# Second block's bias table: rows shifted by a skewed DRAM read in place of a matmul with an exchange matrix

## The reference, cut to what matters

```python
qi = jnp.arange(BLOCK)[:, None]
kj = jnp.arange(2 * BLOCK)[None, :]
dist = qi + BLOCK - kj
bias = rel_bias.astype(jnp.float32)[t5_causal_bucket(dist)]   # (128, 256, 8 heads)
logits = jnp.where(mask, logits + bias, NEG_INF)
```

## Time and profile before

| | |
|---|---|
| median of 3 runs | 2342.88 us |
| the profiled execution's own time | 2340.86 us |
| its span, first to last instruction | 2339.1 us |
| mean granted TensorE clock | 0.995 of full speed |
| PE busy (matmul) | 2297.5 us, 98% of the span |
| DVE busy | 1256.0 us, 54% |
| POOL busy | 859.8 us, 37% |
| ACT busy | 839.3 us, 36% |
| DMA, mean over the span | 93 GB/s |

### The profile page before, as it was taken

The page is one execution under the profiler, slowest core; times in us unless marked ns, Lnnn a source line. Parts: engine busy times, 40 slices in busy tenths (PEclk is TensorE's granted clock), DMA queues, the critical chain, the costliest instruction groups (busy, mean ns, idle before and its releaser), DMA issues.

```text
span 2339.1 us, 28137 instructions
## 1 busy us (share of the span) xinstructions
PE 2297.5 (98%) x11073; PEld 1881.6 (80%) x11073; DVE 1256.0 (54%) x1571; ACT 839.3 (36%) x1014; POOL 859.8 (37%) x200
## 2 busy tenths in 40 slices
PE   7999999999999999999999999999999998999998
PEld 6889777888888888887768888887888777888887
DVE  6677445554436745774455643468555653630533
ACT  5333435332232242333353323222335644422332
POOL 1332223334444443221333444444442333443443
PEclk9999999999999999999999999999999999999999
DMA  6333133454445544331334444445783334444442
GB/s 149 84 68 66 37 73 72 91 107 91 97 100 113 153 104 90 73 69 40 72 70 87 96 96 101 90 111 144 159 168 73 72 73 90 90 90 90 101 106 72
DMA packets 193145, 218.05 MB, mean 93 GB/s; under 512 B 14608, under 2 KB 165272, under 8 KB 192408
## 3 DMA queue, kind: packets, MB, share of 16 engines
q1 hardware_dynamic: 192856, 216.63, 42.3%
q10 hardware_dynamic: 192, 0.05, 0.0%
HBM read 206.92 MB, written 9.73 MB: 93 GB/s over the span
## 4 chain that ended last, share of the span: by engine, by line
PE 49%; issue 34%; POOL 8%; DVE 4%; DMA 1%; SPq 1%; ACT 1%; DVEq 1%; POOLq 0%; ACTq 0%
PE psG L363 15%; PE psG L365 15%; PE psG L364 15%; POOL w_lo L2751 8%; PE psH L650 3%; DMA raw<-in_w_in_dram 1%; SPq L1950 1%; DVE tab L1687 0%; DVE sq L453 0%; PE psH L2142 0%; ACT w_hi L356 0%; PE psH L675 0%; PE psH L2106 0%; DVE s L1687 0%; DMA raw<-in_w_down_dram 0%
## 5 line engine op out<-in xcount | busy, mean ns | idle before, releaser
L2751 POOL TENSOR_TENSOR w_lo<-raw,w_hi 128x2048 fp32r<-128x2048 f32 x184 | 853.0, 4636 | 1459.9 <-ACT w_hi L356 1388.0
L363 PE MATMUL psG<-h_hi,w_hi 128*128 128x512 f32 x1648 | 652.6, 396 | 12.0 <-DVE h_lo L500 7.9
L356 ACT CAST w_hi<-raw 128x2048 fp32r<-128x2048 f32 x184 | 351.0, 1908 | 827.0 <-PE psG L365 797.3
L364 PE MATMUL psG<-h_lo,w_hi 128*128 128x512 f32 x1648 | 643.6, 391 | 0.0
L365 PE MATMUL psG<-h_hi,w_lo 128*128 128x512 f32 x1648 | 643.2, 390 | 0.0
L363 PEld LDWEIGHTS psG<-h_hi,w_hi 128*128 128x128 f32 x1648 | 310.4, 188 | 96.4 <-issue 28.7
L365 PEld LDWEIGHTS psG<-h_hi,w_lo 128*128 128x128 f32 x1648 | 310.3, 188 | 65.6
L364 PEld LDWEIGHTS psG<-h_lo,w_hi 128*128 128x128 f32 x1648 | 310.7, 189 | 64.2 <-issue 1.4
L2688 DVE TENSOR_TENSOR hq<-r 128x512 f32<-128x512 f32 x32 | 84.9, 2691 | 148.8 <-ACT r L2459 148.8
L363 PE MATMUL psG<-hid_hi,w_hi 128*128 128x512 f32 x352 | 138.0, 392 | 1.7 <-POOL w_lo L2751 1.7
L365 PE MATMUL psG<-hid_hi,w_lo 128*128 128x512 f32 x352 | 137.0, 389 | 0.0
(11 more groups left out here) (476 smaller groups left out, 3276.7 us busy)
## 6 DMA issues: line engine op xcount, KB each, us to landing
raw<-in_w_in_dram SPq DMA_DIRECT2D x121, 512.0 KB, 6.4
raw<-in_w_gate_dram SPq DMA_DIRECT2D x44, 512.0 KB, 5.9
raw<-in_w_up_dram SPq DMA_DIRECT2D x44, 512.0 KB, 6.5
raw<-in_w_down_dram SPq DMA_DIRECT2D x32, 512.0 KB, 6.2
raw<-in_w_ff_in_dram SPq DMA_DIRECT2D x32, 512.0 KB, 6.3
raw<-in_w_ff_out_dram SPq DMA_DIRECT2D x32, 512.0 KB, 5.9
raw<-in_w_o_dram SPq DMA_DIRECT2D x16, 512.0 KB, 5.7
raw<-in_w_down_dram SPq DMA_DIRECT2D x16, 384.0 KB, 5.3
```

The costliest lines, as they stand in the source:

```text
L356: act.copy(w_hi[:, s, :], raw[:, s, :]).then_inc(hi_done.sem, 1)
L363: pe.matmul(out, a_hi, b_hi, start=first, stop=False)
L364: pe.matmul(out, a_hi, b_lo, start=False, stop=False)
L2751: pool.tensor_tensor(w_lo[:, s, :], raw[:, s, :], w_hi[:, s, :].bitcast(F32), ALU.subtract)\
```

## The change

The vector is written to DRAM 128 times per head, once for each query row, and the table is read out of that with a row step one word shorter than a row (383 floats in place of 384), so that each row starts one word earlier in the vector. This gives the rows in the right order. The exchange matrix, the read into `t5_up`, the matmuls, the copies and the store of `bias_d` are gone, and with them SP's wait for the small store. The load of `bias` in the second block becomes four DMAs of 256 KB with pieces of 1 KB, in place of two of 512 KB with pieces of 2 KB.

```diff
@@ memory
-    exch = sb("exch", [P, P])
-    t5_dram = nc.dram_tensor("t5_dram", (QH, 3 * P), F32, kind="Internal").ap()
+    t5_dram = nc.dram_tensor("t5_dram", (QH, P, 3 * P), F32, kind="Internal").ap()
-    bias_d = nc.dram_tensor("bias_d", (P, QH * 2 * P), F32, kind="Internal").ap()
-    t5_up = hat("t5_up", 16, [P, QH, 2 * P])
-    bias_s = hat("bias_s", 24, [P, QH, 2 * P])
@@ tables_sync
         if l == 0 and u == 3:
             sp.wait_ge(made_dve.sem, T5_OK)
-            sp.dma_start(t5_dram, t5_rows[:, :]).then_inc(st_t5.sem, 16)
-            sp.wait_ge(st_t5.sem, 16)
-            with nc.allow_non_contiguous_dma(reason="overlapping rows"):
-                sp.dma_start(t5_up[:, :, :], bass.AP(t5_dram.tensor, 0, [[1, P], [3 * P, QH], [1, 2 * P]]))\
-                  .then_inc(ld_t5.sem, 16)
-        if l == 0 and u == 6:
-            sp.wait_ge(made_act.sem, BIAS_OK)
-            sp.dma_start(bias_d, bias_s[:, :, :].rearrange("p h k -> p (h k)")).then_inc(st_bias.sem, 16)
+            sp.dma_start(t5_dram, t5_rows[:, :].unsqueeze(1).broadcast_to([QH, P, 3 * P])).then_inc(st_t5.sem, 16)
@@ tables_stored (ACT, u == 8)
-            act.wait_ge(st_bias.sem, 16)
+            act.wait_ge(st_t5.sem, 16)
@@ tables_pe
         if l == 0 and u == 3:
             pe.wait_ge(ld_c.sem, 64)
-            pe.wait_ge(made_act.sem, BIAS_OK)
...
-        if l == 0 and u == 2:
-            pe.wait_ge(consts.sem, 8)
-            pe.wait_ge(ld_t5.sem, 16)
-            pe.wait_ge(made_dve.sem, ROW_OK)
-            for n in range(4):
-                mm = pe.matmul(psH[:, n, :], exch[:, :], t5_up[:, 2 * n:2 * n + 2, :].rearrange("p a b -> p (a b)"),
-                               start=True, stop=True)
             mm.then_inc(made_pe.sem, 1)
@@ tables_act
-        if l == 0 and u == 2:
-            act.wait_ge(made_pe.sem, FLIP_MM)
-            for n in range(4):
-                act.copy(bias_s[:, 2 * n:2 * n + 2, :].rearrange("p a b -> p (a b)"), psH[:, n, :])
-            act.drain().then_inc(made_act.sem, 1)
@@ input_tables (DVE)
-        dve.wait_ge(st_bias.sem, 16)
+        dve.wait_ge(st_t5.sem, 16)
@@ second_sync
-        sp.wait_ge(st_bias.sem, 16)
+        sp.wait_ge(st_t5.sem, 16)
         for h in range(2):
-            sp.dma_start(bias[:, 4 * h:4 * h + 4, :].rearrange("p (g j) k -> p g (j k)", g=2),
-                         bias_d.rearrange("p (g h jk) -> p h g jk", g=2, h=2)[:, h]).then_inc(ld_bias.sem, 16)
+            for g in range(2):
+                sp.dma_start(bias[:, 4 * h + 2 * g:4 * h + 2 * g + 2, :],
+                             bass.AP(t5_dram.tensor, (4 * g + 2 * h) * P * 3 * P + P - 1,
+                                     [[3 * P - 1, P], [P * 3 * P, 2], [1, 2 * P]])).then_inc(ld_bias.sem, 16)
@@ second_pool (gone, with its call) and second_dve
-        pool.memset(exch[:, :], 0.0).then_inc(consts.sem, 1)
-        pool.wait_ge(consts.sem, 7)
-        pool.affine_select(out=exch[:, :], in_=exch[:, :], compare_op=ALU.not_equal, fill=1.0, base=-(P - 1),
-                           pattern=[[1, P]], channel_multiplier=1).then_inc(consts.sem, 1)
-        dve.wait_ge(ld_bias.sem, 32)
+        dve.wait_ge(ld_bias.sem, 64)
```

More of the change, by code:

```diff
@@ L1515, in build_in @@
     rot_tmp = hat("rot_tmp", 16.5, [P, 2, PAIRS, CH // 2])
[L1517 to L1521, removed]
+    ld_t, ld_c, ld_b, ld_sink, ld_tab = sem("ld_t"), sem("ld_c"), sem("ld_b"), sem("ld_sink"), sem("ld_tab")
+    st_t5, st_tab, st_win, st_wt, st_kern, st_rot = (sem("st_t5"), sem("st_tab"), sem("st_win"), sem("st_wt"),
+                                                     sem("st_kern"), sem("st_rot"))
     made_dve, made_pe, made_act = sem("made_dve"), sem("made_pe"), sem("made_act")
     LOG_OK, T5_OK, ROW_OK, ANG_OK, TAB_OK, E_OK, WT_OK, K_OK, ROT_OK = 1, 2, 3, 4, 5, 6, 8, 10, 11
-    ROW_TR, FLIP_MM, C_TR, WIN_TR, K_MM = 1, 2, 3, 4, 6
-    DT_OK, MAG_OK, BIAS_OK, WIN_OK = 1, 2, 3, 4
+    ROW_TR, C_TR, WIN_TR, K_MM = 1, 2, 3, 5
+    DT_OK, MAG_OK, WIN_OK = 1, 2, 3
     def tables_sync(sp, l, u):
@@ L1617, in tables_pe @@
                                       c_tok[:, r, t, :, :].rearrange("p a b -> p (a b)"), ident[:, :])
-            mm.then_inc(made_pe.sem, 1)
-        if l == 0 and u == 2:
-            pe.wait_ge(consts.sem, 8)
-            pe.wait_ge(ld_t5.sem, 16)
-            pe.wait_ge(made_dve.sem, ROW_OK)
-            for n in range(4):
-                mm = pe.matmul(psH[:, n, :], exch[:, :], t5_up[:, 2 * n:2 * n + 2, :].rearrange("p a b -> p (a b)"),
-                               start=True, stop=True)
             mm.then_inc(made_pe.sem, 1)
@@ L1632, in tables_pe @@
             else:
-                pe.wait_ge(made_act.sem, BIAS_OK)
+                pe.wait_ge(made_act.sem, MAG_OK)
             for i in range(2 * HP):
@@ L2000, in second_sync @@
         sp.wait_ge(st_out.sem, 32 * TB)
-    def second_pool(pool):
-        pool.memset(exch[:, :], 0.0).then_inc(consts.sem, 1)
-        pool.wait_ge(consts.sem, 7)
-        pool.affine_select(out=exch[:, :], in_=exch[:, :], compare_op=ALU.not_equal, fill=1.0, base=-(P - 1),
-                           pattern=[[1, P]], channel_multiplier=1).then_inc(consts.sem, 1)
     r_h2 = rms
@@ L2744, in _ @@
         setup_pool(pool)
-        second_pool(pool)
         def low_parts(first, end):
```

## The result

| | before | after |
|---|---|---|
| median of the runs | 2343.13 us (6 runs, 2342.22 to 2345.55) | 2359.76 us (6 runs, 2356.08 to 2364.18) |
| profiled execution | 2340.86 us | 2356.08 us |
| ratio after / before, 95% interval | | 1.0074 (1.0064 to 1.0083) |

The changed kernel is 0.74% slower. The forecast was 2356.8 us, with a range of 2349 to 2364. The execution that was profiled is the fastest of its six.

A forecast was written before the change was run, and what follows sets the result against it. PE was taken to meet a VectorE chain at the `Et` transposes, so freed matmuls gain nothing; the narrow store delays unit 4, and with the slower clock adds 13.9 us: 2342.88 + 13.9 = 2356.8 us, range 2349 to 2364.

The forecast's parts named there:

- PE's 3.43 us after unit 2: Removing four matmuls after unit 2 of `w_down` frees 3.43 us of PE, only lengthening its VectorE wait before `Et`.
- The chain of waits: Back from PE's 0.77 us wait at 785.76, the last-ending chain runs through VectorE, not the removed matmuls.
- The store is slow: The 1.57 MB broadcast store from 8 partitions runs at 58.5 GB/s and takes 26.9 us; bounds 6.0 and 36.6 us.
- the `Toep` row: Eight `Toep` loads, 16 partitions each in 512-byte pieces, run at 117 GB/s for 18 us; half was taken.
- The estimate from the Trainium skill: Partitions 0 to 7 reach two SBUF ports at 27.2 GB/s each, so the store would take 28.9 us.
- Unit 4 waits behind it: Unit 4's weight load, queued behind the store, lands at 772.0 and is ready at 779.1; PE idle since 762.3.
- The clock: After some 17 us of idling PE restarts at the lower granted clock, adding 1.5 us over units 4 and 5.
- VectorE is no bound afterwards: VectorE has `Et` ready near 782; its transposes start at 799.7 against 785.76, 13.9 us later, and nothing gives that back.
- The bias loads of the second block: Four loads of 1 KB pieces, issued from 1702.90 and first read at 1789.7, cost nothing; bounds 0 and 1 us.
- Rivals 1 and 2: Store over 108 GB/s: 2342.5 us, chance 0.13; with VectorE's chain also ending 3.4 us sooner: 2339.4 us, chance 0.02.
- Rival 3: Weights pass the store on other DMA engines; its landing holds only `Et`, 768 against 769.6: no loss, chance 0.03.
- the break-even: No loss if unit 4 lands at 759.6, meaning a store of 14.5 us or 108 GB/s.

The follow-up runs named there:

- e4: Kernel before, with one of the four exchange matmuls instead of four: 2342.72 us, ratio 1.0006.
- e6: Changed kernel, with the vector stored once (12 KB) in rising order, read in 128 overlapping rows and backwards by VectorE: 2341.08 us, ratio 0.9997.
- e7: Changed kernel, with the vector stored once and read mirrored, and three squaring rounds moved behind `Et`: 2338.12 us, ratio 0.9983.
- e10: Changed kernel, with the store's bytes from partitions 0 to 7 of `hid_hi` instead of `t5_rows`: 2359.21 us, ratio 1.0075.
- e9: Changed kernel, with the store's bytes from partitions 0, 2, .. 14 of `hid_hi`: 2341.57 us, ratio 0.9997.
- e2: Changed kernel, with the store's bytes from partitions 0, 4, .. 28 of `hid_hi`: 2344.39 us, ratio 1.0009.
- e3: Changed kernel, with the same narrow store issued from ScalarE's DMA queue instead of SyncE's: 2360.88 us, ratio 1.0085.
- e1: Changed kernel, with the store's bytes from 128 partitions of `hid_hi` instead of 8: 2343.32 us, ratio 1.0005.

## Why the prediction was right, point by point

- **PE's 3.43 us after unit 2 are gained but worth nothing.** Right in both parts. The stretch before the `c_tok` transposes is 3.39 us shorter, and e4 and e6 show that without the store nothing comes of it. The place was half right: the prediction put the whole longer wait before `Et`, and in e6 1.7 us of it stand before unit 5, through ScalarE, and 1.9 before `Et`. The chain of waits was the right view, the 98% of the page the misleading one. What VectorE's chain was holding back, e7 shows: with its chain shorter, 2.8 us do come back.
- **The store is slow.** Right in kind, and the term was too small: 58.5 GB/s was taken, half of the `Toep` row, and 51 is measured. 1,573 / 51 = 30.8 us instead of 26.9 (an estimate from the window's rate). The estimate from the Trainium skill, 28.9 us, stood between them, still 1.9 short. The prediction's own reason, "the rate falls with the partitions", does not hold as it stands: e10, e9 and e2 have eight partitions each, at 51 to 55 and 101 GB/s and in windows of 267 to 305. What counts is the ways out. Half of the `Toep` row still came near, which fits eight neighbours having half the ways out of sixteen; as a rule on the number of partitions it was luck.
- **Unit 4 waits behind it.** Right. From the mark at unit 0, unit 4 was forecast ready after 48.0 us (779.1 - 731.14) and was after 50.9 (780.23 - 729.38). Of the 2.9 us between, the store's rate is 3.9. Its start makes -0.7: forecast at 9.0 us from the mark, and 8.2 if the landing at 768.42 is counted back by 30.8. No row shows the start itself, so this split rests on the 51 GB/s. The rest is small: from the store's landing to the cast 4.6 us instead of 5.0, cast to ready 7.24 instead of 7.1, GpSimd's operation taking 5.21 instead of 4.61 beside VectorE.
- **The clock.** 1.5 us were added and 1.94 measured. After 19.45 us of idling the granted clock of the window is 0.50, the lower of the two levels, and the matmuls stand 0.43 us apart instead of 0.227 until 784.24.
- **VectorE is no bound afterwards, and nothing gives the time back.** Right: no wait for VectorE before `Et`. The last operation of its first half ends at 775.8, 25 us ahead of the transposes. That is 4.4 us sooner from the mark than the 782 forecast, since with GpSimd idle its six operations took 1.2 us each, where two took over 5 before; nothing hung on it.
- **The bias loads of the second block cost nothing.** Right; four loads of 1 KB pieces, issued from 1719.97, landed within 10.4 us and are first read at 1804.9.
- **The sum.** +13.9 us forecast, +17.4 from mark to mark, +16.6 by the medians. The errors from mark to mark are the unit's 2.9 us, for the most part the store's rate, and half a microsecond in units 4 and 5. Rivals 1 and 2 needed a store above 108 GB/s; e9 at 101 GB/s shows how near the break-even that bound was. Rival 3, weights passing the store, came half true: about half of units 4 and 5 went beside it, as its last sentences had it, and that brought no unit in before the store's landing. e3 shows that a separate queue does not change this.

## What to carry to other kernels

Before a store or load is made larger to save work elsewhere, look at how many groups of neighbouring partitions it touches, and not only at its bytes or the number of partitions: 8 neighbours moved 51 to 55 GB/s here, 8 spread ones 101 or more, and the casts of the weights loaded behind it waited 24 to 29 us for their data, from another queue too. If a broadcast is needed, make it from a small copy in DRAM (8.4 us here for what took some 31, behind a wait for the small store), or avoid it by reading overlapping rows. And before matmuls are removed from a kernel that is 98% busy, follow the chain of waits to the next meeting point with another engine: the removed time counts only if that engine's chain is shortened as well.

## What was not expected of the hardware

- The narrow store held up a load of another queue as it did those of its own: ScalarE waited 23.80 us for unit 3's data in e3.
- The DMA engines are not idle in a narrow transfer, and their share does not show how narrow it is: 0.46 at 55 GB/s and 0.49 at 101.
- A wait of PE of 2 us can be followed by the lower granted clock (0.50 in e9, 0.57 in e4) or not (1.00 in e1 and e2, with waits of 1.6 to 2.0 us).
- The changed kernel's six runs lie 8.1 us apart (2356.08 to 2364.18), those of the kernel before 3.3. But beside e6 to e9, 35 runs of the kernel before lay 9.6 us apart (2338.75 to 2348.32), so the change need not be the reason.
